# Two blocks of a transformer on one core: the first modulation vectors made by TensorE, and the first norm's tokens scaled ahead of them

## The reference

```python
def rms_norm(x, g):
    y = x32 * lax.rsqrt(jnp.mean(x32 * x32, axis=-1, keepdims=True) + EPS)
    return (y * g.astype(jnp.float32)).astype(x.dtype)

def modulate(h, shift, scale):
    return h * (1 + scale) + shift

def ada_params(cond, w_mod, b_mod):
    m = jax.nn.silu(cond) @ w_mod + b_mod
    m = m.reshape(m.shape[:-1] + (N_MOD, 1, D_MODEL))
    return [m[..., k, :, :] for k in range(N_MOD)]
...
        mx = ada_params(c, w_mod[i], b_mod[i])
        x = x + 0.5 * mx[2] * swiglu(modulate(rms_norm(x, norm_g[i, 0]), mx[0], mx[1]),
                                     ffn1_w_gu[i], ffn1_w_d[i])
        if ctx_in_layer:
            my = ada_params(c_ctx, w_mod[i], b_mod[i])
            y = y + 0.5 * my[2] * swiglu(modulate(rms_norm(y, norm_g[i, 0]), my[0], my[1]),
                                         ffn1_w_gu[i], ffn1_w_d[i])
```

## Time and profile before

| | |
|---|---|
| median of 3 runs | 3697.46 us |
| the profiled execution | 3697.62 us |
| its span | 3695.4 us |
| TensorE matmuls busy | 3490.1 us (94% of the span) |
| VectorE busy | 1934.6 us (52%) |
| ScalarE busy | 1252.0 us (34%) |
| GpSimd busy | 361.2 us (10%) |
| mean granted TensorE clock | 0.97 of 2.4 GHz |
| first matmul | 61.97 us |
| first matmul of the feed-forward part | 75.84 us |

### The profile page before, as it was taken

The page is one execution under the profiler, slowest core; times in us unless marked ns, Lnnn a source line. Parts: engine busy times, 40 slices in busy tenths (PEclk is TensorE's granted clock), DMA queues, the critical chain, the costliest instruction groups (busy, mean ns, idle before and its releaser), DMA issues.

```text
span 3695.4 us, 40300 instructions
## 1 busy us (share of the span) xinstructions
PE 3490.1 (94%) x16978; PEld 2876.7 (78%) x16978; DVE 1934.6 (52%) x2662; ACT 1252.0 (34%) x1778; POOL 361.2 (10%) x204
## 2 busy tenths in 40 slices
PE   2999999899979999999999999989999998999998
PEld 2888888787868888788877888766788876678887
DVE  8434343566655453645344333486564648666464
ACT  4322122344433222322233222324442432445242
POOL 3311001111100000000000000320100033010001
PEclk9999999899999999999999999989999999999998
DMA  5423242010115353535222222210232212013221
GB/s 195 142 80 127 86 141 71 34 35 35 35 57 171 126 195 124 182 127 181 91 74 87 96 98 91 89 64 6 69 103 97 97 66 90 6 52 103 97 97 57
DMA packets 95797, 348.81 MB, mean 94 GB/s; under 512 B 10624, under 2 KB 11136, under 8 KB 95104
## 3 DMA queue, kind: packets, MB, share of 16 engines
q1 hardware_dynamic: 94320, 343.06, 27.6%
q10 hardware_dynamic: 1296, 3.18, 0.2%
HBM read 344.10 MB, written 2.10 MB: 94 GB/s over the span
## 4 chain that ended last, share of the span: by engine, by line
PE 84%; DVE 10%; ACT 4%; issue 1%; POOL 1%; DMA 0%; ACTq 0%; DVEq 0%; POOLq 0%
PE PS L343 83%; DVE CAC L1949 2%; ACT G L1160 1%; DVE ST L1755 1%; PE PS L419 1%; DVE WL L1517 1%; DVE X L1928 1%; DVE PTL L1738 1%; DVE G L1619 0%; ACT WH L971 0%; DVE HL L1627 0%; POOL SM L2243 0%; ACT PTH L1141 0%; DVE X L1925 0%; DVE HL L1933 0%
## 5 line engine op out<-in xcount | busy, mean ns | idle before, releaser
L343 PE MATMUL PS<-HH,WH 128*128 128x512 f32 (+1 forms) x3120 | 1193.6, 383 | 38.0 <-DVE HL L1627 16.9
L343 PE MATMUL PS<-HL,WH 128*128 128x512 f32 (+1 forms) x3120 | 1177.8, 378 | 0.0
L343 PE MATMUL PS<-HH,WL 128*128 128x512 f32 (+1 forms) x3120 | 1173.8, 376 | 0.0
L1517 DVE TENSOR_TENSOR WL<-RAW,WH 128x1024 fp32r<-128x1024 f32 x462 | 584.5, 1271 | 766.9 <-ACT WH L971 766.8
L971 ACT ACTIVATE WH<-RAW 128x1024 fp32r<-128x1024 f32 x496 | 522.4, 1057 | 1140.6 <-PE PS L343 1123.0
L343 PEld LDWEIGHTS PS<-HH,WH 128*128 128x128 f32 x3120 | 594.9, 191 | 155.4 <-DVE HL L1627 19.1
L343 PEld LDWEIGHTS PS<-HL,WH 128*128 128x128 f32 x3120 | 594.5, 191 | 109.5 <-issue 5.5
L343 PEld LDWEIGHTS PS<-HH,WL 128*128 128x128 f32 x3120 | 593.6, 190 | 108.8
L343 PE MATMUL PS<-AH,WH 128*128 128x512 f32 x1392 | 526.7, 378 | 1.7 <-DVE WL L1517 1.7
L343 PE MATMUL PS<-AL,WH 128*128 128x512 f32 x1392 | 524.1, 377 | 0.0
L343 PE MATMUL PS<-AH,WL 128*128 128x512 f32 x1392 | 522.9, 376 | 0.0
(11 more groups left out here) (275 smaller groups left out, 3253.9 us busy)
## 6 DMA issues: line engine op xcount, KB each, us to landing
RAW<-wst SPq DMA_DIRECT2D x640, 512.0 KB, 3.3
X<-xT SPq DMA_DIRECT2D x1, 2048.0 KB, 12.2
out<-X SPq DMA_DIRECT2D x8, 256.0 KB, 2.0
PTF<-cb SPq DMA_DIRECT2D x1, 1024.0 KB, 4.7
Y<-yT SPq DMA_DIRECT2D x1, 1024.0 KB, 7.6
PTF<-cb ACTq DMA_DIRECT2D x1, 1024.0 KB, 4.8
HM<-sg ACTq DMA_DIRECT2D x4, 256.0 KB, 3.7
ROPE<-rope SPq DMA_DIRECT2D x1, 512.0 KB, 4.6
```

Source lines behind the costliest of these rows:

```text
L343: return e.matmul(o, l, r, start=start, stop=stop)
L1517: e.tensor_tensor(lo, raw_block(s), f32(hi), ALU.subtract).then_inc(*did("dve_done", ("wlo", b)))
```

## The change

Chunks 0 and 1 of layer 0 are no longer made by the three other engines. Their 16 blocks go to a region of their own, `FM` (64 KB per partition, over `HH`, `HL` and a part of `AH`, which are not in use yet), each with its own semaphore and no buffer to wait for. TensorE takes 128 x 128 pieces of them as weights and two columns, silu(c) and silu(c_ctx) from the small array `CC`, as the moving operand: 16 x 8 fp32 matmuls. VectorE adds the bias and makes the scale (`first_modulation`). The norm's tokens are first multiplied by the statistic into `XN` (`first_norm`), then by the scale, with the shift added, into `G`; ScalarE's part of the norm is now a plain copy. The modulation blocks 18 and 19 come after the norm, together with silu of `CB`. The transfers are reordered.

```diff
@@ TensorE @@
+        def first_modulation():
+            o, _ = hold("mod0", 32, 6, ("modb", 0, 1))
+            q.wait_ge("columns")
+            for j in range(16):
+                descs.extend([(("w_mod", 0, k * 128, j * 128, 128, 128, 0),) for k in range(8)])
+                q.wait_ge("raw", j)
+                for k in range(8):
+                    m = mm(o[:, 2 * j:2 * j + 2], first_block(j)[:, k * 128:(k + 1) * 128], CC[:, 2 * k:2 * k + 2], k == 0, k == 7)
+            m.then_inc(*did("pe_done", ("tile", "mod0")))
...
-        modulation(16)
-        upto["start"] = 17 + NHL - 1
         squares("f00")
-        ffn("f00", norm("f00"))
+        xs = norm("f00")
+        first_modulation()
+        upto["start"] = 18
+        ffn("f00", xs)
@@ ScalarE, norm @@
+            if st == "f00":
+                part(upto[LAST[st]], 1)
             q.wait_ge("mod", l, 3 * i)
...
-                a = e.activation(hi[:, 0:512], s[:, 0:512], ACT.Identity, bias=mcol(l, 3 * i, k, 0))
-                if N > 512:
+                if st == "f00":
+                    a = e.activation(hi, s, ACT.Copy)
+                else:
+                    a = e.activation(hi[:, 0:512], s[:, 0:512], ACT.Identity, bias=mcol(l, 3 * i, k, 0))
+                if st == "at":
...
-                if k >= 2:
+                if k == 3 if st == "f00" else k >= 2:
                     part(upto[LAST[st]], 1)
@@ ScalarE, main @@
+        q.wait_ge("columns in")
+        e.activation(CC[:, :], CC[:, :], ACT.Silu).then_inc(*did("act_done", ("columns",)))
+        for m in range(8):
+            square("in", m)
+        prepare(ACT.Sqrt, "sqrt", "f00")
+        stream(16)
+        norm("f00")
         q.wait_ge("cond in")
         e.activation(CB, CB, ACT.Silu).then_inc(*did("act_done", ("cond",)))
-        for m in range(8):
-            stream(2 * m + 2)
-            if m >= 3:
-                square("in", m - 3)
-        for m in range(5, 8):
-            square("in", m)
-        prepare(ACT.Sqrt, "sqrt", "f00")
-        stream(upto["start"])
-        norm("f00")
         ffn("f00")
@@ VectorE @@
+        def first_modulation():
+            m0, m1 = MOD[:, 0:16], MOD[:, 16:32]
+            q.wait_ge("consts")
+            q.wait_ge("mod zero")
+            q.wait_ge("tile", "mod0")
+            e.tensor_tensor(m1, bank["mod0"][:, 16:32], v1("bm", 16, 16), ALU.add).then_inc(*did("dve_done", ("modb1",)))
+            e.tensor_tensor(m0, bank["mod0"][:, 0:16], v1("bm", 0, 16), ALU.add).then_inc(*did("dve_done", ("modb", 0, 1), ("mod", 0, 0)))
+            q.wait_ge("modb1")
+            e.scalar_tensor_tensor(out=m1, in0=m1, scalar=1.0, in1=v1("ng", 0, 16), op0=ALU.add, op1=ALU.mult).then_inc(*did("dve_done", ("mod", 0, 1)))
...
+        def first_norm(spans, bk):
+            st = "f00"
+            q.wait_ge("tile", ("sp", st))
+            for k in range(8):
+                for src, c, d, kind in spans:
+                    q.wait_ge(kind, "in", k)
+                    e.tensor_tensor(XN[:, k * 768 + c:k * 768 + d], src(k), bk[:, c:d], ALU.mult).then_inc(
...
+            part(upto[LAST[st]], 1)
+            first_modulation()
+            q.wait_ge("mod", 0, 1)
+            for k in range(9):
+                if k < 8:
...
+                        e.tensor_scalar(G(use)[:, c:d], XN[:, k * 768 + c:k * 768 + d], mcol(0, 1, k, s), mcol(0, 0, k, s), ALU.mult, ALU.add).then_inc(
...
+                    e.tensor_tensor(lo, G(use), f32(hi), ALU.subtract).then_inc(*did("dve_done", ("h", st, k - 1), ("gdone", use)))
+                if k == 4:
+                    part(upto[LAST[st]], 1)
@@ SyncE @@
-        e.dma_start(CB, cb).then_inc(*did("cond_in", ("cond in",), by=16))
...
+        e.dma_start(CC[:, :], cc).then_inc(*did("columns_in", ("columns in",), by=16))
+        e.dma_start(Xt[:, :], xT).then_inc(*did("x_in", *[("x", "in", m) for m in range(8)], by=16))
+        e.dma_start(Yt[:, :], yT).then_inc(*did("y_in", *[("y", "in", m) for m in range(8)], by=16))
+            first(0)
+            first(1)
+        e.dma_start(VA[:, :], vec1[:, 0:V1["lam"][0]]).then_inc(*did("consts_in", by=16))
+        e.dma_start(CST[:, :], cst).then_inc(*did("consts_in", ("consts",), by=16))
...
+            for j in range(2, 14):
+                first(j)
+            weights(16)
+            first(14)
+            first(15)
+            weights(17)
+        e.dma_start(CB, cb).then_inc(*did("cond_in", ("cond in",), by=16))
+            weights(18)
+            weights(19)
```

More of the change, by code:

```diff
@@ L131, in wait_ge, with program @@
             self.eng.wait_ge(self.sems[sem], value)
-def program(nc, wst, vec1, vec2, cst, rope, rope96, xT, yT, sg, cb, out, order, old):
+def program(nc, wst, vec1, vec2, cst, rope, rope96, xT, yT, sg, cb, cc, out, order, old):
     ctx = ExitStack()
@@ L971, in stream @@
                     e.activation(split_block(b)[0], raw_block(s), ACT.Copy).then_inc(*did("act_done", ("whi", b)))
-                else:
+                elif order[s][0] == 0 and order[s][1] < 40:
                     l, j = order[s]
[L974 to L979, removed]
+                    q.wait_ge("gprod", l, j)
+                    q.wait_ge("mod zero")
+                    e.activation(PROD, PROD, ACT.Copy, accum_out=mcol(l, j // 8, j % 8, 1)).then_inc(*did("act_done", ("gacc", l, j)))
             pos = max(pos, to)
@@ L1535, in modulation @@
                 q.wait_ge("cond2")
[L1536 to L1548, removed]
+            if l == 0 and ch < 5:
+                q.wait_ge("gprod", l, j)
+            e.tensor_tensor_reduce(raw, raw, CB[:, 0:1024], 1.0, 0.0, ALU.mult, ALU.add, mcol(l, ch, k, 0)).then_inc(*did("dve_done", ("gx", l, j)))
             if k == 7:
@@ L2180, in _ @@
         e.memset(MOD[:, :], 0.0).then_inc(*did("dve_done", ("mod zero",)))
[L2181 to L2185, removed]
+        for m in range(1, 7):
             square_sum(m)
-        stream(upto["start"])
         lam()
+        stream(16)
         norm("f00")
@@ L2225, in stream @@
                         e.tensor_tensor(lo, raw_block(s), f32(hi), ALU.subtract).then_inc(*did("pool_done", ("wlo", b)))
-                else:
+                elif order[s][0] == 0 and order[s][1] < 40:
                     l, j = order[s]
[L2228 to L2236, removed]
+                    q.wait_ge("raw", s)
+                    q.wait_ge("cond")
+                    if product_read:
+                        q.wait_ge("gacc", *product_read)
+                    product_read = l, j
+                    e.tensor_tensor(PROD, raw_block(s), CB[:, 1024:2048], ALU.mult).then_inc(*did("pool_done", ("gprod", l, j)))
             pos = max(pos, to)
@@ new lines, in first, with weights @@
+        def first(j):
+            e.dma_start(first_block(j), wst[j]).then_inc(*did(f"mod_in{j}", ("raw", j), by=16))
+        def weights(d):
+            e.dma_start(raw_block(d), wst[d]).then_inc(*did(f"raw_in{d % NRAW}", ("raw", d), by=16))
+        e.dma_start(CC[:, :], cc).then_inc(*did("columns_in", ("columns in",), by=16))
+        e.dma_start(Xt[:, :], xT).then_inc(*did("x_in", *[("x", "in", m) for m in range(8)], by=16))
+        e.dma_start(Yt[:, :], yT).then_inc(*did("y_in", *[("y", "in", m) for m in range(8)], by=16))
@@ new lines, in _ @@
+        e.dma_start(CB, cb).then_inc(*did("cond_in", ("cond in",), by=16))
+        if nblk:
+            weights(18)
+            weights(19)
+        e.dma_start(ROPE[:, :], rope).then_inc(*did("rope_in", ("rope in",), by=16))
+        for d in range(16 + NRAW, nblk):
+            prev = d - NRAW
+            if order[prev] is None:
+                q.wait_ge("wlo", halves[prev])
+            else:
+                l, j = order[prev]
+                q.wait_ge("gx", l, j)
+                if l == 0 and j < 40:
+                    q.wait_ge("gprod", l, j)
+            weights(d)
@@ L2470, in make @@
                 dt("rope", (128, 1024)), dt("rope96", (128, 1024)), dt("xT", (128, 4096)), dt("yT", (128, 2048)),
[L2471 removed]
+                dt("sg", (2, 128, 1280)), dt("cb", (128, 2048)), dt("cc", (128, 16)), dt("out", (128, 4096), "ExternalOutput"))
         return nc, *program(nc, *args, order, old)
     descs = make([], None)[1]
[L2475 removed]
+    order = [tuple(d[1:]) if d and d[0] == "T" else ("P", n) if d and d[0][0] == "w_mod" else None for n, d in enumerate(descs[::UPB])]
     nblk = len(order)
```

68 lines of the change are left out of this document (33 added, 35 removed).

## The result

The changed kernel takes 3720.85 us (median of 6 runs, 3709.32 to 3722.65) against 3697.06 for the kernel before (6 runs, 3693.45 to 3703.94): ratio 1.0055, 95% interval 1.0039 to 1.0072. Run again in the session of the first experiments the ratio was 1.0049 (1.0037 to 1.0062), 19.6 us between the medians. The forecast was 3710 us, 12.6 more than before, range 3690 to 3717: the direction and the mechanism were right, the size was too small and the time lies above the range.

A forecast was written before the change was run, and what follows sets the result against it. TensorE's matmuls bound the kernel from 120 to 640 us, so only the start could move: S 6.4 us later plus 6.2 more from S to U, 12.6 on 3697.62, gives 3710 us, range 3690 to 3717.

The forecast's parts named there:

- U: Start of the second `u` tile on TensorE, after ScalarE's first silu; 108.34 us before, forecast at S + 38.7.
- the fast moment: At the start of the 128 narrow matmuls: clock seemingly raised briefly by the spread, 1.5 us taken off their 54.6.
- S: Start of the feed-forward part on TensorE; 75.84 us before, forecast 82.2, 6.4 later.
- When the statistic is ready: Program start: transfers, squares, sums, root and spread, after which the new matmuls start at 26 us.
- The 128 matmuls: TensorE's narrow stream: 256 records at the slow pace of 0.213 us, 54.6 us less 1.5, ending at 79.1.
- rival A: Narrow stream: the clock opens, 256 records take 31.2 us instead of 54.6, time 3688, faster; chance 0.14.
- From there to S: From the matmuls' end to S: small operations on MOD, `G`, copy and difference, 3.1 us against 3.5 before.
- From S to U: From S to U: norm, silu of CB, three pairs of products and splits, 38.7 us, 6.2 more than 32.5.
- B: Between S and U: third pair of products hidden, clock low, only S moves by 6.4, time 3704; chance 0.12.
- C: As forecast, but products collide with VectorE, +3, 3713, or squares' stage later, +2 to 4; forecast included, chance 0.70.
- D: Narrow stream: TensorE waits for chunks, though the last is due at 33 us; given no chance of its own.
- The second edit: First norm: tokens times statistic into XN, then scale and shift into `G`, plain copy on ScalarE; 0.4 us at S.

The follow-up runs named there:

- the first experiments: Follow-up runs after the first comparison; in their session the changed kernel ran once more without an edit, ratio 1.0049 to the kernel before.
- the run with silu alone: Changed kernel with only silu of CB moved ahead of the norm, blocks 18 and 19 left behind it; one execution, U at 121.91 us.
- swapped: Changed kernel with the chunks as moving operand (128 columns) and the two vectors as weights, result turned by sixteen small matmuls; ratio 0.9985 to the kernel before.
- wide ones: Changed kernel with six unused bf16 matmuls of 512 columns ahead of each chunk's narrow ones; ratio 1.0041 to the kernel before.
- half the matmuls: Changed kernel with four of each chunk's eight pieces multiplied, 64 matmuls instead of 128; ratio 0.9974 to the kernel before.
- both repairs: Changed kernel with operands swapped, and silu of CB with blocks 18 and 19 ahead of the norm; ratio 0.9959 to the kernel before.

## Why the prediction was right in kind and too small

**The step that failed** is the sizing of the sum; path, waits and pace were as said. The measured median is 10.6 us over the forecast (3697.62 + 12.6). 6.0 of them stand ahead of U: the start of the 128 matmuls (+1.8), the fast moment taken off (+1.5), the way to S (+0.3) and the term S to U (+2.4, chiefly the norm's end, put at S + 9.3 and measured at S + 10.9). The other 5.2 (less 0.6, since the median of the kernel before came out lower) are behind U, where the sum has no term at all: the runs show a scatter of 12 us there, and in the first comparison it went against the change. The 18.6 us at U alone would have given 3715.6, inside the range; that the time lies above it needed the scatter too, which is chance as far as these runs tell.

- **What bounds, and U as the measure.** Right: 592.90 and 592.96 us from U to the attention's first matmul, and TensorE is busy in all 510 us from 130 to 640. But the forecast of the time took the rest as fixed, and it isn't.
- **When the statistic is ready.** Forecast 26 for the new matmuls, measured 27.80. The transfers ran at 410 GB/s in the stretch of the earlier trace rows, which has 437 (row below), and Y, 3.1 MB behind the start, was there at 11.48 instead of 10.7. ScalarE's squares had the forecast's 0.83 us, but VectorE's sums beside them take 1.05 each (16.03, 17.08, 18.14 in the chain), more than the squares: they, not the squares, end last, at 19.1 instead of 17.3. The step "the sums keep step" failed, +1.8; already the forecast's own 0.95 is more than its 0.83. From there to the spread all agrees (5.26 and 0.6).

```profile
5.00:10.00 5.00, 0.00 (x0) 1.00 0.97 410
```

- **The 128 matmuls.** The term that decides, and right: 0.213 a record, 54.61 us, against the 31.2 of rival A. The 1.5 us taken off for a fast moment was wrong for this execution (it had none) and half of what others had (3.1). Either has been seen, so no fixed term fits it: +1.5 here. By the advice of the Trainium skill ("TensorE: Matmul & The Clock Gate", Why this matters for your kernels) to keep TensorE continuously busy this stream should have had the full clock; the trace does not agree: 54.61 us without a gap at 0.213 a record.
- **From there to S.** Forecast 3.1, measured 3.4 (82.41 to 85.81). S: 82.2 forecast, 85.81 measured; 1.8 + 1.5 + 0.3 are the 3.6.
- **From S to U.** Forecast 38.7, measured 41.10, within the bounds of 32.5 and 41.5. In the forecast's own steps: the norm's last copy ends at S + 10.9, not S + 9.3. The 9.3 was wrong in itself: five tiles at its own 0.75 + 1.0, one more `G` and the copy give some 10.3. A tile then took 1.65 instead of 1.75 (0.5 less), and VectorE's split of block 17 (1.14, at 90.61), which I had not counted, stands among the tiles; table and silu of CB 3.45 to the first product (3.4 forecast); first pair 7.26 (7.2); from there splits, second pair and transfer 11.4 to 118.83 (11.6 forecast, with the transfer alone 3.3 instead of 2.5); third pair 7.2; and the first silu of the feed-forward part itself, 0.85 to U, which I had put "within my rounding". So 1.6 + 0.85 make up the 2.4: a slip, a split and a silu left out, not a mechanism missed. The wait before the second `g` tile is 6.83, not 3 to 4, and adds nothing, as was said and as the run with silu alone shows.
- **Sum.** Forecast +12.6 at U, measured +18.57. Nearly every miss went the same way.
- **Rivals.** A is refuted by the 54.61 us; but its price was right: once the clock is granted (swapped, wide ones) a record takes 0.114 to 0.115, and with the operands swapped U is 3.1 us earlier than before. B is refuted: the added pair stands in the chain with 7.3 us, and U - S grew by 8.6. Of C the squares' part came true. D is refuted by half the matmuls taking half the time (24.20 us and the 3.1 of a fast moment, against 54.61).
- **The second edit.** Forecast: 0.4 at S, and 3.4 for the norm's end on ScalarE behind S. Measured 0.7 and 4.5 in the changed kernel, 0.8 and 2.0 with both repairs, and a loss of 3.1 where nothing covers its sixteen products.

Not settled: what in the narrow matmuls keeps the clock low. The runs show that it stays at 1.2 GHz in a stream of two moving columns without gaps and is at 2.4 GHz with 128, or with wide ones between; which property decides wasn't separated (the swap changes the weights' columns too). That stream's level is read from the pace, 0.213, in the first execution, and from the clock itself, 0.50, in the second.

## What to carry to other kernels

Price a stream of narrow matmuls by the number of records times the pace that such matmuls had before in this program, and look whether they hold the clock themselves; if they don't, turn the operands so that the long side moves, and count the turn back. When work leaves the head of a program for an engine that was idle, ask what else the head was hiding: here a pair of products and a silu that had been ahead of the norm became 9.2 us of the chain behind it, and the new stream, beside which VectorE, GpSimd and ScalarE stood mostly idle, was the place for them. And read a start-up change by an instant behind which nothing differs, since the total's scatter can be as large as the effect.

## What was unexpected of the hardware

- Useless work made a stretch faster: with 96 more wide matmuls a chunk took 3.00 us instead of 3.41, and S came 2.6 to 5.7 us earlier (but the time, ratio 1.0041 against 1.0049, isn't clear of the noise).
- The clock raised for a moment after the spread comes in some executions and not in others of the same kernel (51.5 or 54.6 us for the same 256 records).
- The same 1914 records of attention took 323.47 us at a mean clock of 0.98 and 327.77 at 0.95, in two executions of the same kernel.
